# Eight cached sequences in one decoder step: one column tile of TensorE per token, joined window loads, unrolled code

## The chip, the core and the metric

The kernel runs on one NeuronCore of a Trainium2 chip. The metric is the device time of one launch in microseconds (us). The core has TensorE (matrix products; PE in the rows, with its weight loads on a line of their own, PEld), VectorE (DVE), ScalarE (ACT), GpSimd (POOL) and SyncE (SP), whose instruction stream issues most of the DMA transfers. Each engine runs its own instructions in order, and engines wait for each other on semaphores.

## What is computed

One layer of a decoder step for a prompt of 256 tokens and for 8 cached sequences of 4 new tokens each (32 sample tokens). A combined projection gives the inputs of four branches; their outputs are projected, gated and summed, and a gated convolutional MLP follows. The change is in the two attention branches of the 8 cached sequences:

```python
# branch A, group g of three, (window, dilation) = (128,1), (512,4), (2048,16), 2 heads each
kk = concatenate([buf[:, :, 0], k], 1); vv = concatenate([buf[:, :, 1], v], 1)   # cache: W rows x (k,v) x 2 x 128
idx = W + t - j * dilation                                # token t sees taps j = 0..window/dilation
logits = q . kk[idx] + bias[j]; p = softmax over the taps; o = p . vv[idx]
o_A = sum over the groups, weighted by the softmax of their log-sum-exps
# branch B, 4 heads, 1024 cached keys in 8 pages of 128 rows, found through page_table
s = q . mean(keys of a block of 256); the 3 best of 4 blocks stay; softmax over them and the own keys
o_B = p . v
```

All data are f32. Per sequence 8 key pages and 8 value pages of 256 KB each are read, and 1.75 MB of window caches.

## The kernel before

**Order of the whole.** The input projection (about 30 to 316 us), the two small branches C and D, the prompt's attention (to 406 us), then the 8 cached sequences (to 624 us), then gates, output projection and MLP, in which TensorE works without a pause.

**A sequence, on TensorE** (`sample`, L1704). Keys come from the cache with the token on the partition, so every 128x128 piece is turned (`turn`, L1467: a transpose against `ident`) and copied from PSUM by ScalarE (bank 0) or VectorE (bank 1) before it can be multiplied. One sequence issues, in this order: the window keys turned (L1714 to L1733); own-key products of B (L1735) and A (L1742); the first two key groups of the *next* sequence turned (`keys`, L1745); the sliding branch's scores (L1752, L1757, L1761); three more key groups; B's scores of the next sequence, first half (L1695); a key group; the weights `L_b` of B turned, 9 pieces (L1774); two key groups; the weights `L_a` of A turned, 6 pieces (L1782); B's product with the values (L1798); A's (L1804 to L1812); B's result turned (L1819); B's scores of the next sequence, second half; A's result turned (L1826).

**One row set for A.** The sliding branch keeps its 2 heads x 4 tokens as 8 rows. With dilation 4 or 16 token t sees other rows of the cache than token t', so `qs_a` and `pt_a` hold 8 columns for each (head, residue) with zeros where the token does not belong, and 8 products add up into `ps[0:8, 6]`:

```python
for h in range(2):
    for r in range(4):
        c = 48 + 8 * (4 * h + r)
        e.matmul(ps[0:8, 6, 128:256], qs_a[:, c:c + 8], kt_a[:, h, r * P:r * P + P], start=h + r == 0, stop=h + r == 4)
```

B keeps its 4 heads in 4 groups of 32 PSUM partitions, `ps[32 * h:32 * h + 32, ...]`, with 32 weight columns each.

**VectorE and ScalarE.** VectorE's order in a sequence (L1216 to L1288): the copy of window keys, block sums (L1230), scale and bias of B's logits (L1232), the short window's keys (L1221), a key group of the next sequence, the choice of blocks (L1244 to L1250) and the maximum (L1252), A's logits and maximum (L1256 to L1261), and only then the copy of the next sequence's fourth key group (L1264), on which TensorE's L1695 waits. ScalarE copies the even key groups, does the exponentials and scales the results.

**Loads** (`sample_loads`, L502). SyncE reads each page number from SBUF (`value_load`, L481) and issues one DMA of 256 KB (L483), 16 in a sequence. Windows are read in 6 DMAs, 3 for keys and 3 for values (L489 to L493), in rows of 1 KB, into single buffers. The order in a round of the loop is: window keys, 8 key pages of the next sequence, 8 value pages, window values.

**Loop.** Sequences 0 to 6 run as a hardware loop on each engine with counts in registers, the last one as a copy behind it. Ahead of it TensorE makes the bias rows (L1658, L1653) with f32r operands, VectorE copies them to SBUF, and only then (L1670) the first keys are turned.

Of the kernel before, what the change touches and what calls it, by code (L numbers as in the profile page):

```python
# [23 lines left out]
P = 128  # L24
# [111 lines left out]
def build(nc, known, d, o, ctx):  # L136
# [65 lines left out]
    QA = 176  # L202
    qpad_a = sb("qpad_a", [P, NB, QA], F32, R_RAW)
    kv = [sb(f"kv{s}", [P, 4, 512], F32, R_Z + 8192 * s) for s in range(6)]
    bias_b = sb("bias_b", [P, PAST + NB * NS], F32, R_SPLIT)
    bias_a = sb("bias_a", [8, 320 + NB * 96], F32, R_SPLIT + 5120)
# [3 lines left out]
    L_a = sb("L_a", [8, 416], F32, R_SPLIT + 26496)  # L210
    pt_b = sb("pt_b", [P, 9, B_HEADS, 32], F32, R_SPLIT + 9472)
    pt_a = sb("pt_a", [P, 8 + 32 + 32 + 24], F32, R_SPLIT + 28192)
    ob = sb("ob", [P, P], F32, R_SPLIT + 28576)
    oa = sb("oa", [8, 256], F32, R_SPLIT + 29088)
# [50 lines left out]
    win0 = keep("win0", [P, 512])  # L265
    qs_b = keep("qs_b", [P, B_HEADS, 32])
    qs_a = keep("qs_a", [P, QA])
# [26 lines left out]
    kv_landed = [sem(f"kv_landed{s}") for s in range(6)]  # L294
    win_landed = [[sem(f"win{w}_{x}_landed") for w in (1, 2, 0)] for x in ("keys", "values")]
# [56 lines left out]

    def sample_steps(i, last):

        def name(x):
            return ("last", x) if last else x

        def at(count, x, back=0):
            if not last:
                return count.at(x, i, back=back)  # L360
            return count.at(x, NB - 2) if back else count.at(("last", x))
        return name, at


    @block.sync
    def _(sp):
# [106 lines left out]

        sp.wait_ge(pe.sem, pe.at(("PV", NU - 1)))
        sp.wait_ge(dve.sem, dve.at(("P", NU - 1)))
        sp.wait_ge(pool.sem, pool.at("z_own"))
        sp.wait_ge(landed["pages"], 16)

        def page_loads(n, cache, half, slot):
            for q in range(4):  # L480
                page = sp.value_load(pages[0:1, bass.ds(n * NPG + (4 * half + q), 1)], min_val=0,  # L481
                                     max_val=cache.shape[0] - 1)
                sp.dma_start(kv[slot][:, q:q + 1, :], cache[bass.ds(page, 1)].rearrange("a p h e -> p a (h e)"))\  # L483
                    .then_inc(kv_landed[slot], 16)

        def window_loads(i, v):

            cols = slice(256 * v, 256 * v + 256)
            sp.dma_start(kv[2][:, :, cols], d["cache_win1"][0, bass.ds(i, 1), :, v]  # L489
                         .rearrange("a (p r) h e -> p (a r) (h e)", r=4)).then_inc(win_landed[v][0], 16)  # L490
            sp.dma_start(kv[3][0:64, :, cols], d["cache_win2"][0, bass.ds(i, 1), :, v]
                         .rearrange("a (p r) h e -> p (a r) (h e)", r=16)[:, 0:4, :]).then_inc(win_landed[v][1], 16)
            sp.dma_start(win0[:, cols], d["cache_win0"][0, bass.ds(i, 1), :, v].rearrange("a p h e -> p (a h e)"))\  # L493
                .then_inc(win_landed[v][2], 16)

        def next_keys(i, half):

            need = i * 8 + (4 * half + 4)
            if not isinstance(i, int):
                need = sp.snap(sp.to_reg(need))  # L500
                sp.wait_ge(landed["pages"], 16)
            sp.wait_ge(keys_turned, need)  # L502
            page_loads(i + 1, d["cache_k"][0], half, half)

        def sample_loads(i, first, last):
            def used(x):

                return pe.at(x, NB - 2) if last else pe.at(x, i, back=1)
            if not first:
                sp.wait_ge(pe.sem, used(("kTa", 3)))  # L510
            window_loads(i, 0)
            if not last:
                next_keys(i, 0)
                next_keys(i, 1)
            if not first:
                need = used("pv_b")
                if not last:
                    need = sp.snap(sp.to_reg(need))
                    sp.wait_ge(landed["pages"], 16)
                sp.wait_ge(pe.sem, need)  # L520
            for half in range(2):
                page_loads(i, d["cache_v"][0], half, 4 + half)
            if not first:
                sp.wait_ge(pe.sem, used("pv_a"))
            window_loads(i, 1)
        for half in range(2):
            page_loads(0, d["cache_k"][0], half, half)
        sample_loads(0, True, False)
        with sp.Fori(1, NB - 1) as i:
            sample_loads(i, False, False)  # L530
        sample_loads(NB - 1, False, True)


        sp.wait_ge(q_put, 2 * NB)
        with sp.Fori(0, 4) as i:
            for b in range(4):
                for j in range(4):
# [49 lines left out]
    def _(e):  # L587
# [68 lines left out]
        with e.Fori(1, NB) as i:  # L656
            sample_queries(i)
# [1290 lines left out]
```

## Time and profile before

| | us |
|---|---|
| median of 3 runs | 2175.45 (2171.96 to 2177.34) |
| the profiled execution | 2177.7 |
| its span, first to last instruction | 2175.9 |
| TensorE busy, products | 2037.1 (94%) |
| TensorE busy, weight loads | 1927.0 (89%) |
| VectorE busy | 1073.0 (49%) |
| ScalarE busy | 740.7 (34%) |
| GpSimd busy | 81.9 (4%) |

The profiled execution is one run with the hardware profiler; it lasted 1.8 us longer than its span. Its mean granted TensorE clock was 0.969 of full speed. Products are pipelined, so that the busy times of neighbours overlap, and a row's start is a better mark than its end. In the timeline rows an f32 product appears as two records (passes), a transpose as one; "x16" for L1752 is 8 products.

DMA issues in the page: 64 of `cache_k` and 64 of `cache_v` with 256 KB each, and of `cache_win` 16 with 512 KB, 16 with 256 KB and 16 with 128 KB. For one of the 8 sequences that is 16 x 256 + 2 x (512 + 256 + 128) KB = 5888 KB, 6.03 MB.

### The profile page before, as it was taken

The numbers are of one execution on the slowest core, as the hardware profiler recorded it, in microseconds if no ns is written. First come the engines' busy times: TensorE is split into PE (matmuls) and PEld (weight loads), VectorE is DVE, ScalarE is ACT, GpSimd is POOL, SyncE is SP. The second block draws the span as 40 slices with busy tenths as digits, with TensorE's granted clock in tenths as the row PEclk, the third lists the DMA queues.
The fourth block names the chain that finished last, engine by engine and source line by source line (L and its number), as shares of the span: only waits on it lengthen the run. The fifth ranks groups of instructions, "written<-read, shape, count | busy, mean of one in ns | idle before, by whom it ended". The sixth has DMA issues, their size and how long they took to land.

```text
span 2175.9 us, 37737 instructions
## 1 busy us (share of the span) xinstructions
PE 2037.1 (94%) x15329; PEld 1927.0 (89%) x15329; DVE 1073.0 (49%) x1078; ACT 740.7 (34%) x618; POOL 81.9 (4%) x170
## 2 busy tenths in 40 slices
PE   7999996788989999999998969999999999999995
PEld 5999984555569999999998959999999999999994
DVE  4333325434444434444443375656655665665564
ACT  4333332322233333433332424333333333333332
POOL 0000002000000000000000011000000000000001
PEclk9999997899999999999999989999999999999998
DMA  6545522389865454544546514555665565666532
GB/s 233 170 157 171 188 63 72 114 247 244 231 198 170 150 174 157 164 161 159 166 164 193 173 39 156 173 165 193 213 211 206 205 215 202 217 207 216 198 135 59
DMA packets 190741, 377.03 MB, mean 173 GB/s; under 512 B 9849, under 2 KB 34705, under 8 KB 189114
## 3 DMA queue, kind: packets, MB, share of 16 engines
q1 hardware_dynamic: 184412, 340.50, 49.0%
q10 hardware_dynamic: 6247, 35.31, 4.1%
q8 instruction: 66, 1.08, 0.2%
q14 instruction: 16, 0.13, 0.0%
HBM read 365.43 MB, written 37.66 MB: 185 GB/s over the span
## 4 chain that ended last, share of the span: by engine, by line
PE 89%; DVE 5%; ACT 2%; issue 2%; SPq 1%; DMA 1%; ACTq 0%; DVEq 0%
PE ps L1486 26%; PE ps L1488 26%; PE ps L1487 26%; PE ps L1468 4%; PE ps L1474 1%; DVE m_T L1031 1%; PE ps L1798 1%; PE ps L1806 1%; PE ps L1809 1%; PE ps L1695 1%; PE ps L1752 1%; PE ps L1812 1%; PE ps L1637 0%; DVE w_lo L1014 0%; DVE stat L1024 0%
## 5 line engine op out<-in xcount | busy, mean ns | idle before, releaser
L1014 DVE TENSOR_TENSOR w_lo<-w_raw,w_hi 128x2048 fp32r<-128x2048 f32 (+1 forms) x272 | 614.7, 2261 | 786.2 <-ACT w_hi L700 786.2
L1486 PE MATMUL ps<-xn_hi,w_hi 128*128 128x288 f32 x3104 | 917.5, 296 | 27.6 <-DVE xn_lo L1037 13.8
L1488 PE MATMUL ps<-xn_hi,w_lo 128*128 128x288 f32 x3104 | 918.8, 296 | 0.0
L1487 PE MATMUL ps<-xn_lo,w_hi 128*128 128x288 f32 x3104 | 916.9, 295 | 0.0
L700 ACT ACTIVATE w_hi<-w_raw 128x2048 fp32r<-128x2048 f32 (+1 forms) x272 | 514.4, 1892 | 1042.4 <-PE ps L1488 1029.4
L1486 PEld LDWEIGHTS ps<-xn_hi,w_hi 128*128 128x128 f32 x3104 | 585.3, 189 | 32.0 <-DVE xn_lo L1037 15.4
L1487 PEld LDWEIGHTS ps<-xn_lo,w_hi 128*128 128x128 f32 x3104 | 585.1, 189 | 0.0
L1488 PEld LDWEIGHTS ps<-xn_hi,w_lo 128*128 128x128 f32 x3104 | 585.1, 189 | 0.0
L1486 PE MATMUL ps<-act_hi,w_hi 128*128 128x288 f32 x704 | 207.9, 295 | 2.8 <-DVE act_lo L1387 2.8
L1488 PE MATMUL ps<-act_hi,w_lo 128*128 128x288 f32 x704 | 208.5, 296 | 0.0
L1487 PE MATMUL ps<-act_lo,w_hi 128*128 128x288 f32 x704 | 207.9, 295 | 0.0
L1486 PEld LDWEIGHTS ps<-act_hi,w_hi 128*128 128x128 f32 x704 | 132.8, 189 | 3.0 <-DVE act_lo L1387 3.0
L1487 PEld LDWEIGHTS ps<-act_lo,w_hi 128*128 128x128 f32 x704 | 132.8, 189 | 0.0
L1488 PEld LDWEIGHTS ps<-act_hi,w_lo 128*128 128x128 f32 x704 | 132.7, 188 | 0.0
L1394 DVE TENSOR_TENSOR m_T<-ps,m_T 128x1152 f32<-128x1152 f32 x44 | 59.6, 1354 | 54.7 <-PE ps L1488 54.7
L1371 DVE SCALAR_TENSOR_TENSOR hc<-H,conv,hc 128x304 f32<-128x304 f32 x176 | 82.2, 529 | 0.0
L1486 PE MATMUL ps<-M_hi,w_hi 128*128 128x288 f32 x256 | 76.7, 300 | 5.5 <-DVE w_lo L1014 5.5
L1488 PE MATMUL ps<-M_hi,w_lo 128*128 128x288 f32 x256 | 76.7, 300 | 0.0
L1487 PE MATMUL ps<-M_lo,w_hi 128*128 128x288 f32 x256 | 76.6, 299 | 0.0
L1468 PE MATMUL ps<-ident,kv 128*128 128x128 f32 (+1 forms) x384 | 54.8, 282 | 13.4 <-DVE kt_a L1221 6.8
L1468 PEld LDWEIGHTS ps<-ident,kv 128*128 128x128 f32 (+1 forms) x384 | 41.0, 146 | 29.0 <-issue 12.8
L1488 PE MATMUL ps<-O_hi,w_lo 128*128 128x288 f32 x224 | 66.1, 295 | 0.0
(269 smaller groups left out, 1534.7 us busy)
## 6 DMA issues: line engine op xcount, KB each, us to landing
w_raw<-in_w_in SPq DMA_DIRECT2D x104, 1024.0 KB, 5.0
w_raw<-in_w_up SPq DMA_DIRECT2D x88, 1024.0 KB, 5.1
w_raw<-in_w_down SPq DMA_DIRECT2D x44, 1024.0 KB, 5.1
kv<-in_cache_k SPq DMA_DIRECT2D x64, 256.0 KB, 3.5
kv<-in_cache_v SPq DMA_DIRECT2D x64, 256.0 KB, 3.0
w_raw<-in_w_o SPq DMA_DIRECT2D x16, 1024.0 KB, 5.1
out<-in_cache_win ACTq DMA_DIRECT2D x32, 512.0 KB, 4.3
kv<-in_cache_win SPq DMA_DIRECT2D x16, 512.0 KB, 6.4
```

The lines of the kernel that those rows point to most:

```text
L700: e.activation(w_hi[s][:, 0:k, 0:n], w_raw[slot][:, 0:k, 0:n], ACT.Copy).then_inc(hi_ready, 1)
L1014: e.tensor_tensor(w_lo[s][:, 0:k, 0:n], w_raw[slot][:, 0:k, 0:n], w_hi[s][:, 0:k, 0:n].bitcast(F32), ALU.subtract).then_inc(lo_ready, 1)
L1031: e.scalar_tensor_tensor(out=dst[:, c, :], in0=src[:, c, :], scalar=gains[:, g + c:g + c + 1], in1=stat[:, 2, :], op0=ALU.mult, op1=ALU.mult)\
L1371: e.scalar_tensor_tensor(out=dst, in0=src, scalar=w[tap], in1=dst, op0=ALU.mult, op1=ALU.add)\
L1394: e.tensor_tensor(m_T[:, 4 * j:4 * j + 4, :], ps[:, 4 * (j % 2):4 * (j % 2) + 4, 0:TOK], m_T[:, 4 * j:4 * j + 4, :], ALU.add).then_inc(y_a ...
L1468: return e.transpose(dst, src, ident[0:n, 0:n])
L1474: mm = e.matmul(ps[:, bank, 0:TOK], ones[:, :], sq[:, q, k, :], start=q == 0 and k == 0, stop=q == 3 and k == 3)
L1486: e.matmul(dst, w_hi[s][:, r, cols], x_hi[:, k0 + r, :], start=first and r == 0, stop=False)
L1487: e.matmul(dst, w_hi[s][:, r, cols], x_lo[:, k0 + r, :], start=False, stop=False)
L1488: mm = e.matmul(dst, w_lo[s][:, r, cols], x_hi[:, k0 + r, :], start=False, stop=last and r == k - 1)
L1695: mm = e.matmul(ps[32 * h:32 * h + 32, 4 + half, :], qs_b[:, h, :], kt_b[:, half, h, :], start=True, stop=True)
L1752: e.matmul(ps[0:8, 6, 128:256], qs_a[:, c:c + 8], kt_a[:, h, r * P:r * P + P], start=h + r == 0, stop=h + r == 4)
```

## The change

1. **Column tiles.** A's rows move to 4 groups of 32 partitions, one per token, with head h in row 32t + h. Scores, weights times values and the biases each go out as 4 products with 32 weight columns, one per group: own keys 24 products for 6, scores 24 for 18 (8 + 8 + 8 for 8 + 8 + 2), values 16 for 12. `L_a`, `oa`, `bias_a` have 128 partitions for 8. The own values of the three groups are gathered on 96 partitions (`v_own_a`).
2. **Turns of weights.** The turns of `L_b`, `L_a`, `ob`, `oa` become ordinary f32 products against 16, 8 or 4 chosen columns of `ident`; their PSUM rows hold only what is copied on. The pieces of `L_a` are 4 for 6. B's 9 pieces go to one bank, and ScalarE alone copies them.
3. **Loads.** A window is one DMA for keys and values (3 for 6 in a sequence, rows of 2 KB, four in a row for the dilated ones), with two sets of buffers. Keys have 3 half buffers for 2. The first 8 key pages are issued during the prompt's attention. Weights of the next stage load from the end of A's values in sequence 6.
4. **Unrolled.** All 8 sequences are written out on every engine; there is no loop and no register in the waits. GpSimd builds `qs_a` from `z_own` in each sequence.
5. **Start.** A's biases are f32 products in column tiles; TensorE turns the first keys with no wait for VectorE's copies. B's own-key product moves up, between the window's turns.

```diff
-    kv = [sb(f"kv{s}", [P, 4, 512], F32, R_Z + 8192 * s) for s in range(6)]
+    def window_buffers(name, win1_at, win2_at, win0_at):
...
+    k_half = [sb("k_half0", [P, 4, 512], F32, R_Z + 32768), sb("k_half1", [P, 4, 512], F32, R_Z + 40960),
+              sb("k_half2", [P, 4, 512], F32, R_RAW + 16384)]
+    v_half = [sb(f"v_half{s}", [P, 4, 512], F32, R_Z + 8192 * s) for s in range(2)]
...
+        def key_loads(j):
+
+            if j >= 2 * NB:
+                return
+            if j >= 3:
+                sp.wait_ge(keys_turned, 4 * (j - 3) + 4)
+            page_loads(j // 2, d["cache_k"][0], j % 2, k_half[j % 3], k_landed[j % 3])
+
+        def value_loads(n):
+            if n:
+                sp.wait_ge(pe.sem, pe.at(("pv_b", n - 1)))
...
+        def window_loads(n):
...
+            if n >= 2:
+                sp.wait_ge(pe.sem, pe.at(("pv_a", n - 2)))
+            w0, w1, w2 = windows[n % 2]
+            sp.dma_start(w1[:, :, :], d["cache_win1"][0, n].rearrange("(p r) v h e -> p r (v h e)", r=4))\
+                .then_inc(win_landed[n % 2][1], 16)
...
+        sp.wait_ge(dve.sem, dve.at(("oc", 2)))
+        sp.wait_ge(pool.sem, pool.at("z_own"))
+        sp.wait_ge(landed["pages"], 16)
+        key_loads(0)
+        key_loads(1)
         sp.wait_ge(pe.sem, pe.at(("PV", NU - 1)))
         sp.wait_ge(dve.sem, dve.at(("P", NU - 1)))
...
+        sp.wait_ge(pe.sem, pe.at("bias"))
+        window_loads(0)
+        key_loads(2)
+        key_loads(3)
+        value_loads(0)
+        key_loads(4)
+        window_loads(1)
+        for n in range(1, NB):
+            key_loads(2 * n + 3)
+            key_loads(2 * n + 4)
+            value_loads(n)
+            window_loads(n + 1)
...
-            for h in range(2):
-                for r in range(4):
-                    c = 48 + 8 * (4 * h + r)
-                    e.matmul(ps[0:8, 6, 128:256], qs_a[:, c:c + 8], kt_a[:, h, r * P:r * P + P],
-                             start=h + r == 0, stop=h + r == 4)
...
+            for h in range(HPG):
+                for t in range(NT):
+                    e.matmul(ps[32 * t:32 * t + 32, 6, 128:256], qs_a[:, 1, h, t, :], kt_a[:, h, t * P:t * P + P],
+                             start=h == 0, stop=h == 1, skip_group_check=True)
...
-                turn(ps[:, 7 if pg < 4 else 3, pg % 4 * P:pg % 4 * P + P], L_b[:, pg * P:pg * P + P], P)
...
+                e.matmul(ps[:, 3, 16 * pg:16 * pg + 16], L_b[:, pg * P:pg * P + P], row_b,
+                         start=True, stop=True)
...
-            e.matmul(ps[0:8, 6, 0:256], pt_a[:, 0:8], win0[:, 256:512], start=True, stop=False)
-            for r in range(4):
-                e.matmul(ps[0:8, 6, 0:256], pt_a[:, 8 + 8 * r:16 + 8 * r], kv[2][:, r, 256:512],
-                         start=False, stop=False)
...
+            for t in range(NT):
+                e.matmul(ps[32 * t:32 * t + 32, 6, 0:256], pt_a[:, 0, t, :], w0[:, 256:512],
+                         start=True, stop=False, skip_group_check=True)
+            for t in range(NT):
+                e.matmul(ps[32 * t:32 * t + 32, 6, 0:256], pt_a[:, 1, t, :], w1[:, t, 256:512],
+                         start=False, stop=False, skip_group_check=True)
```

How the order moves, at three places of TensorE's stream. Rows with MATMUL name what is written, the moving and the weight operand (`kv_87`, `kv_88` and `k_half_...` are key buffers), and weight columns x moving columns; ISA and REGISTER_ALU rows are the loop's register work.

Scores of the sliding branch, to B's first scores of the next sequence. Before:

```order
L1752 MATMUL ps<-kt_a,qs_a 8x128 x8
L1757 MATMUL ps<-kt_a,qs_a 8x64 x8
L1761 MATMUL ps<-kt_a,qs_a 8x128 x2
L1679 ISA
L1468 MATMUL ps<-ident,kv_87 128x128 x8
L1679 REGISTER_ALU
L1468 MATMUL ps<-ident,kv_88 128x128 x4
L1691 ISA
L1693 REGISTER_ALU
L1695 MATMUL ps<-kt_b,qs_b 32x512 x4
L1468 MATMUL ps<-ident,kv_88 128x128 x4
L1711 ISA
```

With the change:

```order
L1707 MATMUL ps<-kt_a,qs_a 32x128 x8
L1713 MATMUL ps<-kt_a,qs_a 32x64 x8
L1718 MATMUL ps<-kt_a,qs_a 32x128 x8
L1433 MATMUL ps<-ident,k_half_88 128x128 x8
L1433 MATMUL ps<-ident,k_half_86 128x128 x4
L1660 MATMUL ps<-kt_b,qs_b 32x512 x4
L1433 MATMUL ps<-ident,k_half_86 128x128 x4
```

The scores go from 18 products with 8 weight columns to 24 with 32; what follows is unchanged in order.

The turns of the weights, before:

```order
L1468 MATMUL ps<-ident,L_b 128x128 x4
L1773 REGISTER_ALU
L1468 MATMUL ps<-ident,L_b 128x128 x4
L1468 MATMUL ps<-ident,L_b 32x128
L1679 REGISTER_ALU
L1468 MATMUL ps<-ident,kv_88 128x128 x8
L1711 ISA
L1468 MATMUL ps<-ident,L_a 128x8 x2
L1468 MATMUL ps<-ident,L_a 64x8
L1468 MATMUL ps<-ident,L_a 32x8 x3
```

With the change:

```order
L1727 MATMUL ps<-ident,L_b 128x16 x8
L1729 MATMUL ps<-ident,L_b 32x16
L1433 MATMUL ps<-ident,k_half_86 128x128 x8
L1735 MATMUL ps<-ident,L_a 128x8 x2
L1735 MATMUL ps<-ident,L_a 64x8
L1735 MATMUL ps<-ident,L_a 96x8
```

Each turned piece now has 16 or 8 moving columns for 128 or fewer; next keys stay between the two groups.

The sliding branch's values and the results, before:

```order
L1804 MATMUL ps<-win_151,pt_a 8x256
L1806 MATMUL ps<-kv_89,pt_a 8x256 x4
L1809 MATMUL ps<-kv_90,pt_a 8x256 x4
L1812 MATMUL ps<-v_own,pt_a 8x256 x3
L1711 ISA
L1468 MATMUL ps<-ident,ob 128x128
L1688 REGISTER_ALU
L1695 MATMUL ps<-kt_b,qs_b 32x512 x4
L1711 ISA
L1468 MATMUL ps<-ident,oa 128x8 x2
```

With the change:

```order
L1752 MATMUL ps<-win_even,pt_a 32x256 x4
L1755 MATMUL ps<-win_even,pt_a 32x256 x4
L1758 MATMUL ps<-win_even,pt_a 32x256 x4
L1761 MATMUL ps<-v_own_a,pt_a 32x256 x4
L1766 MATMUL ps<-ident,ob 128x16
L1660 MATMUL ps<-kt_b,qs_b 32x512 x4
L1772 MATMUL ps<-ident,oa 128x4 x2
```

12 products of 256 columns become 16, and B's scores of the next sequence stay between the two results.

## Rows read from the trace of the kernel before

**Rows 1.** The core's engines in six stretches: length, busy time (instructions) of each, TensorE clock, DMA share, GB/s.

```profile
424.75:455.87 31.12, 24.50 (x241) 14.25 (x237) 11.06 (x26) 6.29 (x13) 0.54 (x2) 0.89 0.87 251
455.87:480.17 24.30, 21.70 (x239) 13.73 (x237) 11.37 (x28) 6.29 (x13) 0.53 (x2) 1.00 0.88 246
552.93:578.09 25.16, 23.30 (x238) 14.56 (x238) 11.55 (x28) 6.30 (x13) 0.53 (x2) 0.93 0.89 245
557.65:561.00 3.35, 3.35 (x15) 2.19 (x16) 2.06 (x6) 0.00 (x0) 0.00 (x0) 0.50 0.77 229
602.39:623.60 21.21, 17.03 (x191) 11.24 (x190) 8.88 (x24) 4.14 (x9) 0.00 (x0) 0.92 0.86 291
700.00:900.00 200.00, 196.28 (x1477) 195.60 (x1477) 87.63 (x45) 71.77 (x43) 0.00 (x0) 1.00 0.50 163
```

**Rows 2.** TensorE in order of time, third sequence: start, length, line, operation, tiles, idle before and releaser.

```profile
482.66 0.51 PE L1742 MATMUL ps<-z_own,qs_a 128*8 128x32 f32 x12
...
484.74 0.66 PE L1468 MATMUL ps<-ident,kv 128*128 128x128 f32 x4 [0.97 <-DVE kt_a L1221]
485.32 1.92 PE L1752 MATMUL ps<-kt_a,qs_a 128*8 128x128 f32 x16
487.07 1.06 PE L1757 MATMUL ps<-kt_a,qs_a 128*8 128x64 f32 x16
487.97 0.60 PE L1761 MATMUL ps<-kt_a,qs_a 128*8 128x128 f32 x4
...
491.54 1.06 PE L1695 MATMUL ps<-kt_b,qs_b 128*32 128x512 f32 x8 [1.04 <-DVE col L1266]
...
493.03 1.15 PE L1468 MATMUL ps<-ident,L_b 128*128 128x128 f32 x9
...
494.98 0.40 PE L1468 MATMUL ps<-ident,L_a 8*128 8x8 f32 x6
495.30 1.95 PE L1798 MATMUL ps<-kv,pt_b 128*32 128x128 f32 x64
...
497.54 0.60 PE L1804 MATMUL ps<-win,pt_a 128*8 128x256 f32 x2
...
503.00 0.33 PE L1468 MATMUL ps<-ident,ob 128*128 128x128 f32 x1
```

**Rows 3.** VectorE in order of time, same sequence.

```profile
485.43 0.69 DVE L1213 COPY kt_b<-ps 128x512 f32<-128x512 f32 x1 [0.75 <-PE ps L1468]
...
490.54 0.67 DVE L1213 COPY kt_b<-ps 128x512 f32<-128x512 f32 x1
```

**Rows 4.** TensorE in order of time, bias products ahead of the sequences.

```profile
415.75 0.48 PE L1468 MATMUL ps<-ident,kv 128*128 128x128 f32 x1 [1.90 <-DVE bias_b L1206]
```

**Rows 5.** TensorE in order of time, first sequence.

```profile
446.21 1.02 PE L1804 MATMUL ps<-win,pt_a 128*8 128x256 f32 x2 [4.02 <-DMA win<-in_cache_win]
447.02 3.62 PE L1806 MATMUL ps<-kv,pt_a 128*8 128x256 f32 x8
```

**Rows 6.** TensorE in order of time, spatial-gating branch at a clock of 0.50.

```profile
360.00 1.75 PE L1601 MATMUL ps<-wd,vc_tok 32*128 32x32 f32 x8
```

**Rows 7.** TensorE in order of time, last sequence.

```profile
611.82 1.74 PE L1468 MATMUL ps<-ident,L_b 128*128 128x128 f32 x9 [3.20 <-ACT L_b L845]
```

**Rows 8.** SyncE's DMA issues in order of time, inside the loop.

```profile
502.55 8.46 SPq L483 DMA_DIRECT2D kv<-in_cache_v  x8
```

**Rows 9.** SyncE's DMA issues in order of time, the unrolled last sequence.

```profile
596.49 7.96 SPq L483 DMA_DIRECT2D kv<-in_cache_v  x8
604.49 0.58 SPq L489 DMA_DIRECT2D kv<-in_cache_win  x1
...
605.79 0.60 SPq L493 DMA_DIRECT2D win<-in_cache_win  x1
```

**Rows 10.** DMA queues between 430 and 456 us.

```profile
q8 instruction: 2, 0.03, 0.6%
```

More of the change, by code:

```diff
@@ L351, in ffn_unit @@
         return unit_no(U_FFN - 4, 12, i, j)
[L353 to L362, printed above, removed]
     @block.sync
@@ L496, in next_keys @@
[L496 to L525, printed above, removed]
@@ L1763, in sample @@
-            mm.then_inc(pe.sem, pe.step(name("s_a")))
-            if not last:
-                keys(nxt, 2, 5, at)
-                scores(nxt, 0, at)
-                keys(nxt, 5, 6, at)
-            need = value(at(act, "E_b"))
-            e.wait_ge(pool.sem, pool.at("ident"))
-            e.wait_ge(act.sem, need)
-            for pg in range(8):
-                if pg == 4:
-                    e.wait_ge(dve.sem, at(dve, "o_a", back=1))
-                turn(ps[:, 7 if pg < 4 else 3, pg % 4 * P:pg % 4 * P + P], L_b[:, pg * P:pg * P + P], P)
@@ L1775, in sample @@
-            turn(ps[0:NS, 2, P:2 * P], L_b[:, PAST:PAST + NS], P).then_inc(pe.sem, pe.step(name("ptb")))
-            if not last:
-                keys(nxt, 6, 8, at)
-            need = value(at(act, "E_a"))
-            e.wait_ge(pool.sem, pool.at("ident"))
-            e.wait_ge(act.sem, need)
-            turn(ps[:, 6, 416:424], L_a[:, 0:128], 8)
-            turn(ps[:, 6, 424:432], L_a[:, 128:256], 8)
-            turn(ps[0:64, 6, 432:440], L_a[:, 256:320], 8)
-            for g in range(3):
-                mm = turn(ps[0:NS, 6, 440 + 8 * g:448 + 8 * g], L_a[:, 320 + 32 * g:352 + 32 * g], 8)
@@ L1818, in sample @@
-            e.wait_ge(act.sem, need)
-            turn(ps[:, 2, 256:384], ob[:, :], P).then_inc(pe.sem, pe.step(name("otb")))
-            if not last:
-                scores(nxt, 1, at)
-            need = value(at(act, "oa"))
-            e.wait_ge(pool.sem, pool.at("ident"))
-            e.wait_ge(act.sem, need)
-            for h in range(2):
-                mm = turn(ps[:, 2, 432 + 8 * h:440 + 8 * h], oa[:, h * P:h * P + P], 8)
-            mm.then_inc(pe.sem, pe.step(name("ota")))
-        keys(0, 0, 8, None)
@@ L1838, in _ @@
+            mm.then_inc(pe.sem, pe.step(("ota", n)))
+        keys(0, 0, 8)
+        scores(0, 0)
+        scores(0, 1)
+        for n in range(NB):
+            sample(n)
         with e.Fori(0, 4) as i:
```

538 lines of the change are left out of this document (257 added, 281 removed).

## The prediction

> **What bounds the kernel now.** The change touches only the stretch of the eight sequences, 424.75 to 623.6 us, and the bias products ahead of it. I first cut that stretch by sequence [rows 1]: the first takes 31.12 us, a steady one 24.30, the sixth 25.16, the last 21.21. TensorE is busy for 21.7 of 24.3 us, VectorE for 11.4, the DMA engines for 0.88 of the time. So TensorE's order of work sets the pace, with two idle gaps of note in each sequence [rows 2]: 0.97 us before the second key group, on VectorE's copy of window keys, and 1.04 before B's first scores at 491.54, on VectorE again. The second gap ends a chain: VectorE starts on the second key group at 485.43 and works without a wait to the fourth, at 490.54 [rows 3]. From 491.54 on TensorE waits for almost nothing until VectorE's chain can start again with the next window keys. A sequence is therefore one part at VectorE's pace and one at TensorE's, and only what shortens the second part shortens the sequence.
>
> The queue behind them is nearly as full. A round of SyncE has 16 page issues and 6 window issues; it takes 8.46 us from the first to the last of 8 value pages in the loop and 7.96 in the unrolled copy [rows 8, 9].
>
> **Part by part, in a steady sequence.**
>
> *Values of the sliding branch.* Before: 497.54 to 503.00, 5.46 us for 12 products of 256 columns, one behind the other [rows 2]. After: four rounds of four column tiles. The same form stands in the trace: B's 32 products with 128 columns take 1.95 us in rounds of four heads, 0.244 a round; twice the columns give 0.49, and four rounds 1.95. **-3.5 us**, in TensorE's part.
>
> *Scores.* Before 3.2 us (485.32 to 488.5: 487.97 and about 0.53 of its row). After: two rounds of 128 columns, two of 64, two of 128: 1.2. The 2.0 us won lie inside VectorE's chain: the fourth key group still waits for it, and the gap before B's scores grows from 1.04 to about 3.0. **0.** The own-key products of A grow from 6 to 24, in six rounds; they have the 0.97 gap behind them, so even twice their 0.45 us (row 482.66 [rows 2]) costs **0**; were that gap gone, 0.5.
>
> *Turns of the weights.* A turn costs 0.115: from 493.03 to 494.98 there are 17 [rows 2]. An f32 product has two passes, each with a weight load of 128 columns. The nearest row is 8 such passes with 32 moving columns in 1.75 us at half clock [rows 6]: 0.22 a pass, 0.11 at full clock. So `L_b` takes 8 x 0.22 + 0.1 = 1.9 against 1.0, `L_a` (128, 128, 64 and 96 weight columns) about 0.7 against 0.32, `oa` 0.44 against 0.23. **+1.5 us**, all in TensorE's part. The bounds are 0 (a product for a turn at the same price) and twice that.
>
> *Copies.* ScalarE takes over VectorE's share of `pt_b`, two copies of some 0.25 us; two key groups and the turns of `L_a`, 1.7 us, cover them. VectorE has one copy of results for two and four of `pt_a` as before. GpSimd's query copies follow the scores of the sequence before, a whole sequence ahead. **0.**
>
> A steady sequence at full clock: 24.3 - 3.5 + 1.5 = **22.3 us**.
>
> *The clock.* What TensorE did before it fell: after an idle gap of 4.02 us, 8 passes of A's values took 3.62 us [rows 5], where a full clock needs 1.8 (5.46 x 8 / 24); after 3.20 the 9 turns took 1.74 instead of 1.15 [rows 7, 2]; and in the sixth sequence the clock stood at 0.50 for 3.35 us [rows 1], after key turns, little products and the 0.97 gap. There it cost 25.16 - 24.30 = 0.86, because half of the 1.7 us lost ran inside the second gap. With the change, some 5 us of turns and idling (gap 3.0) come right before TensorE's own part, where nothing hides a spell. I take one spell in every other sequence, 1.7 / 2 = **+0.85**: 23.15 us. The Trainium skill (TensorE: Matmul & The Clock Gate, PE-mode transpose) says that transposes do not count as busy for the clock in the same way; by that the new stretch counts as idle throughout, every sequence has its spell, and the rival below holds. The sixth sequence agrees with it, the five without a spell do not settle it.
>
> *SyncE and DMA.* The round is 16 x 1.09 + 1.9 for three window issues = 19.4 us [rows 9], under 22.3; three key halves and two window sets let it run ahead. The waits put into the queue (keys turned, B's values, A's values of two sequences before) hold back only what stands behind them there, and each is over when SyncE gets to it, save the first rounds. DMA: 6.03 MB a sequence at the main stage's 163 GB/s for a share of 0.50, 326 GB/s, is 18.5 us; at the loop's 246 for 0.88 it is 21.6. Either is below 22.3, the second barely.
>
> *The ends.* Keys start with no wait for VectorE's bias copies: 1.90 us idle go [rows 4], two turns and slower f32 biases add 0.8: **-1.1**. The first sequence loses its wait for window values (4.02) and the half clock after it: 31.12 to 23.15, **-8.0**. Sequences 2 to 7: 602.39 - 455.87 = 146.5 to 138.9, **-7.6**. The last: -3.5 + 1.5, and the gap before its turns grows from 3.2 to 5.2, with 0.3 more at half clock: **-1.7**. The next stage's weights are asked for some 20 us before the end of the sequences and need about 10: 0.
>
> **Sum:** -1.1 - 8.0 - 7.6 - 1.7 = -18.4 us on 2177.7. The median of the runs is 2175.45, 2.3 lower; against it I forecast **2157 us**.
>
> **The rivals.**
> - *Full clock throughout* (0.20). The loop's other sequences had it in spite of 2.6 us idle. Then 22.3 us each: -1.1 - 8.8 - 12.7 - 2.0 = -24.6, 2151 us.
> - *A spell in every sequence* (0.18). 24.0 us each: -1.1 - 7.1 - 2.5 - 1.3 = -12.0, 2163 us. The gap of 3.0 is near the 3.20 of [rows 7].
> - *The loads become the bound* (0.08). At the loop's 251 GB/s [rows 1] 6.03 MB take 24.0 us and TensorE waits for values: again about 2163. For it speaks the share of 0.88; against it, that this rate was what TensorE and SyncE asked for, and that rows of 2 KB replace rows of 1 KB.
> - *Slower, by the clock* (0.06). The stretch falls to half and does not recover at once, since turns and gaps go on. At full clock the change is worth 24.6 us, 3.1 a sequence, so it turns when a sequence spends over 6.2 us of TensorE's part at half. With 10 us it loses 5.0 each: -24.6 + 40 = +15, 2191 us.
> - *Unrolled code starves TensorE* (0.02). In 26 us of the first sequence two instruction packets show, at 0.6% of 16 engines 1.25 us each [rows 10]. A sequence has about 600 TensorE instructions; two or three exposed fetches of 1.25 and a queue as long would make it 26 to 28 us: +30, 2205. The Trainium skill (Runtime: NRT & Kernel Launch, Instruction fetch mechanics) says that the sequencer fetches ahead in blocks of 256 instructions and that the cost is mostly hidden; by it this rival gives nothing. The unrolled last sequence shows no such stall.
> - *The tiles do not run side by side*: 16 products of 0.455 are 7.3 us for 5.46, scores 5 for 3.2: some 29 us a sequence, 2215. B's rows in the same form speak against it; it is within the last 0.02.
> - *No measurable change* (0.04): several small losses eat the 18 us.
>
> **The numbers.** Forecast 0.42. Faster by over 0.3% (6.5 us, about what a measurement can tell here): 0.42 + 0.20 + 0.18 + 0.08 = 0.88; within it 0.04; slower 0.08. Low end: full clock, and half of the 1.5 us for the turns not paid (8 x 0.75 = 6), 2145. High end: a spell each and the turns dearer by 0.75, 2170. That leaves out the slower cases and most of "no change".
>
> **What would show it.** Steady sequences of 22.3 us, or 24.0 with a spell of 0.50 in them; A's values 2.0 us; the turns of `L_b` 1.9; an idle gap of some 3 us before B's first scores, ended by VectorE; the first sequence no longer than the others; SyncE's rounds with room between them. A wait for a DMA in steady sequences, turns of `L_b` over 2.5 us, or a gap of another length before B's scores would prove me wrong.

## The result, and the profile after

The changed kernel takes **2187.95 us** (median of 6 runs, 2184.24 to 2189.77) against 2176.94 (median of 6, 2171.96 to 2178.78) on the same chip: ratio 1.0051, 95% interval 1.0036 to 1.0066. It is slower by 11 us where 18 were to be won. The profiled execution lasted 2189.3 us, its span 2187.6 (before 2175.9), its mean granted TensorE clock 0.955 (before 0.969). One run of experiment 7 below, of 2882.75 us at a mean clock of 0.646, is left out of its median.

Each experiment was measured beside the kernel before, on its own chip (medians there 2177.5 to 2178.8), and its ratio is to that kernel. The changed kernel was not repeated there, and the intervals are about 4 us wide to each side, so differences of a few us between two experiments are not told apart.

The stretch of the sequences cut into sequences, from the first own-key product of B of one to that of the next (length, busy time with instructions of PE, PEld, DVE, ACT, POOL, TensorE clock, DMA share, GB/s):

```profile
421.46:448.73 27.27, 23.23 (x307) 17.74 (x306) 11.06 (x25) 6.62 (x15) 0.57 (x3) 0.81 0.94 288
...
530.59:557.87 27.28, 23.17 (x308) 17.74 (x307) 11.05 (x25) 6.57 (x15) 0.57 (x3) 0.81 0.75 224
...
585.13:612.41 27.28, 23.17 (x307) 17.72 (x306) 11.06 (x25) 6.56 (x15) 0.57 (x3) 0.81 0.49 144
```

All seven take 27.3 us with a clock of 0.81, where before five took 24.16 to 24.30 at 1.00 (one of them in [rows 1]). The last of these rows moves only 144 GB/s, since the pages run out there, and is as long as the first with 288: loads are not the bound. The same view of the second sequence, one microsecond a row:

```profile
458.00:459.00 1.00, 0.13 (x4) 0.16 (x8) 0.84 (x3) 1.00 (x5) 0.00 (x0) 1.00 0.66 274
459.00:460.00 1.00, 1.00 (x9) 0.16 (x5) 0.00 (x0) 0.43 (x1) 0.00 (x0) 1.00 1.01 344
460.00:461.00 1.00, 1.00 (x7) 1.00 (x7) 0.13 (x1) 0.00 (x0) 0.00 (x0) 0.53 1.15 311
...
469.00:470.00 1.00, 1.00 (x26) 0.94 (x20) 0.00 (x0) 0.00 (x0) 0.00 (x0) 0.50 0.92 277
470.00:471.00 1.00, 1.00 (x32) 0.65 (x24) 0.00 (x0) 0.00 (x0) 0.00 (x0) 0.85 0.82 260
471.00:472.00 1.00, 1.00 (x24) 0.42 (x16) 0.00 (x0) 0.37 (x1) 0.00 (x0) 1.00 0.90 328
```

The clock falls at about 460.1 and is back at 470.3: **10.2 us at half clock** (0.50 in the rows), with TensorE busy all the time. I call such a stretch a spell. Each of the seven sequences has one. What TensorE does in it, in order of time (start, length, line, operation, tiles, idle before and releaser):

```profile
452.28 0.66 PE L1433 MATMUL ps<-ident,k_half 128*128 128x128 f32 x4 [1.00 <-DVE kt_a L1202]
452.86 0.65 PE L1707 MATMUL ps<-kt_a,qs_a 128*32 128x128 f32 x16
453.32 0.41 PE L1713 MATMUL ps<-kt_a,qs_a 128*32 128x64 f32 x16
453.55 0.62 PE L1718 MATMUL ps<-kt_a,qs_a 128*32 128x128 f32 x16
...
458.87 1.06 PE L1660 MATMUL ps<-kt_b,qs_b 128*32 128x512 f32 x8 [2.71 <-issue]
459.87 0.97 PE L1433 MATMUL ps<-ident,k_half 128*128 128x128 f32 x4
460.63 3.43 PE L1727 MATMUL ps<-ident,L_b 128*128 128x16 f32 x16
463.99 0.29 PE L1729 MATMUL ps<-ident,L_b 128*32 128x16 f32 x2
464.21 1.97 PE L1433 MATMUL ps<-ident,k_half 128*128 128x128 f32 x8
465.98 1.59 PE L1735 MATMUL ps<-ident,L_a 128*128 128x8 f32 x8
467.50 3.30 PE L1747 MATMUL ps<-v_half,pt_b 128*32 128x128 f32 x64
...
471.08 0.64 PE L1752 MATMUL ps<-win_odd,pt_a 128*32 128x256 f32 x8
...
473.22 0.39 PE L1766 MATMUL ps<-ident,ob 128*128 128x16 f32 x2
```

The sliding branch's scores take 1.24 us (452.86 to 454.10), so the gap ahead of B's first scores, 1.04 before [rows 2], is 2.71. The releaser is given as "issue", but VectorE's copy of the fourth key group ended just ahead (VectorE in order of time; [rows 3] before):

```profile
458.09 0.68 DVE L1194 COPY kt_b<-ps 128x512 f32<-128x512 f32 x1
```

B's scores still run at full clock, and the fall comes within the key group behind them (0.97 us for 0.66). The turns of `L_b` as products, two key groups, the turns of `L_a` and most of B's values run at half. A's values, after the spell, take 2.14 us (471.08 to 473.22) against 5.46.

Time at half clock is counted below in one way for every kernel: the granted clock of 420 to 620 us in steps of 0.5 us, each step's share under 1.00 taken twice. A spell that an edge of the stretch cuts counts with what lies inside. Before it is **14.8 us**, after **71.7**. A microsecond at half does half a microsecond's work, so that 56.9 us more are worth some 28 us. Expected and measured change of the profiled execution differ by 18.4 + 11.6 = 30.

### The profile page after: what moved, and what is told of

Its sections match the earlier page's. It is cut to its first block, busy times and chain, and to the rows that moved or that the text cites. A ratio compares the mean times of both kernels' runs of the same rounds, so it can differ in the third digit from the quotient of the medians.

```text
span 2187.6 us, 38132 instructions
## 1 busy us (share of the span) xinstructions
PE 2041.9 (93%) x15921; PEld 1953.5 (89%) x15921; DVE 1068.8 (49%) x1049; ACT 743.5 (34%) x628; POOL 80.5 (4%) x170
## 4 chain that ended last, share of the span: by engine, by line
PE 90%; DVE 5%; issue 2%; ACT 2%; ACTq 0%; DMA 0%; SPq 0%; DVEq 0%
PE ps L1451 26%; PE ps L1453 26%; PE ps L1452 26%; PE ps L1433 4%; PE ps L1747 1%; PE ps L1727 1%; PE ps L1439 1%; DVE m_T L1018 1%; PE ps L1660 1%; PE ps L1735 1%; DVE col L1212 0%; PE ps L1602 0%; DVE L_b L1214 0%; DVE w_lo L1001 0%; DVE stat L1011 0%
## 5 line engine op out<-in xcount | busy, mean ns | idle before, releaser
L1452 PE MATMUL ps<-O_lo,w_hi 128*128 128x288 f32 x224 | 66.0, 294 | 0.0
L1451 PE MATMUL ps<-O_hi,w_hi 128*128 128x288 f32 x224 | 65.9, 294 | 0.0
```

Of the source, the lines that this page charges most:

```text
L1451: e.matmul(dst, w_hi[s][:, r, cols], x_hi[:, k0 + r, :], start=first and r == 0, stop=False)
L1452: e.matmul(dst, w_hi[s][:, r, cols], x_lo[:, k0 + r, :], start=False, stop=False)
```

## The experiments

Theory A: column-tiled scores end early, TensorE idles 2.7 us in VectorE's chain, and the clock falls there. Theory A2: the products that replaced the turns keep it from coming back. Rivals: the products alone do it; or something else (loads, unrolled code) takes the time and the clock is a side show. All experiments but the sixth start from the changed kernel.

**1. The gap filled with products.** `ones` times `ident` into unused columns, whose results nobody reads.

```diff
             if n + 1 < NB:
+                for k in range(11):
+                    e.matmul(ps[:, 7, 256:384], ones[:, :], ident[:, :], start=True, stop=True)
                 scores(n + 1, 0)
```

> The changed kernel with 11 extra f32 products of ones by the identity (128 columns each, some 2.4 us at full clock, into PSUM columns that nobody reads) in TensorE's gap ahead of B's first scores, in sequences 1 to 7. The outputs stay the reference's. Theory A (the idle gap of 2.7 us, with turns around it, drops the clock, and the 10 us at half clock behind it cost the time): the clock stays at 1.00 in steady sequences, the turns of L_b take 1.9 us for 3.4, a sequence takes 22.2 to 22.5 us for 27.3, and the kernel some 33 to 38 us less than the changed one: about 2152. Theory B (the new products that turn the weights, 128 weight columns against 16 moving ones, are slow or drop the clock by themselves, whatever the gap): turns of L_b still 3.4 us, 27.3 us a sequence, about 2188.

2162.63 us (2160.60 to 2164.82), ratio to the kernel before 0.9927 (0.9910 to 0.9943). Sequences, by the same view; five of seven stand at 1.00:

```profile
469.01:491.59 22.58, 20.93 (x329) 15.78 (x328) 11.05 (x25) 6.55 (x15) 0.58 (x3) 1.00 1.01 329
...
537.59:561.79 24.20, 22.56 (x330) 17.14 (x329) 11.05 (x25) 6.56 (x15) 0.57 (x3) 0.93 0.80 227
```

More work on TensorE makes the kernel 25 us faster, less than the 33 to 38 expected. Time at half clock: 27.3 us. So the clock was most of the loss, and without the idle gap most sequences have no spell. A sequence of the change at full clock is 22.58 us.

The gap is not the only thing that goes before a spell. The sixth and seventh sequences, filled like the others, have one of 3.4 us each. In the sixth it begins at 553.0, with B's values, 5.3 us behind the last idle piece, which was 0.26 us long (TensorE in order of time):

```profile
547.73 1.07 PE L1660 MATMUL ps<-kt_b,qs_b 128*32 128x512 f32 x8 [0.26 <-issue]
...
553.02 3.43 PE L1749 MATMUL ps<-v_half,pt_b 128*32 128x128 f32 x64
```

**2. `L_b` turned by transposes again.** The nine turns as before, VectorE copying its share; the gap stays. `L_a`'s pieces move to another bank.

```diff
-                e.matmul(ps[:, 3, 16 * pg:16 * pg + 16], L_b[:, pg * P:pg * P + P], row_b,
-                         start=True, stop=True)
+                turn(ps[:, 7 if pg < 4 else 3, pg % 4 * P:pg % 4 * P + P], L_b[:, pg * P:pg * P + P], P)
```

> The changed kernel with one part undone: L_b is turned by 9 transposes of 128 columns into two banks again, and VectorE copies its share of pt_b. The gap stays. [...] Rival (the length of the spell has nothing to do with the form of the turns; transposes do no more for the clock): the spell stays about 10 us and only the turns' own 0.9 us at full clock, up to 1.8 at half, are won: 25.5 to 26.5 us a sequence, about 2178.

2157.47 us (2155.06 to 2159.91), ratio 0.9902 (0.9885 to 0.9918); 34.1 us at half clock. In its third sequence, TensorE in order of time:

```profile
483.16 1.20 PE L1663 MATMUL ps<-kt_b,qs_b 128*32 128x512 f32 x8 [2.71 <-issue]
484.29 1.12 PE L1436 MATMUL ps<-ident,k_half 128*128 128x128 f32 x4
485.19 2.13 PE L1436 MATMUL ps<-ident,L_b 128*128 128x128 f32 x9
487.12 1.17 PE L1436 MATMUL ps<-ident,k_half 128*128 128x128 f32 x8
...
489.04 1.96 PE L1751 MATMUL ps<-v_half,pt_b 128*32 128x128 f32 x64
```

Behind the same gap the clock falls (nine turns in 2.13 us for 1.15), but it is back by 487, after 3.42 us. Of six spells in 420 to 620, one lasts 10.2. Two sequences have the gap of 2.71 and no spell at all; they take 21.56 us at 1.00.

The run is faster than the 2165 to 2172 us that I had put beside theory A2. Some 8 us of its gain on the change are the turns' own price, 22.58 - 21.56 in each sequence, and not the clock.

**3. The gap shortened from the other side.** VectorE's copy of the fourth key group moves ahead of the two maxima and A's logits.

```diff
+            odd_keys(n + 1, 3)
...
-            odd_keys(n + 1, 3)
```

> The changed kernel with VectorE's copy of the fourth key group put ahead of the maximum of B's logits and of A's logits, behind the choice of blocks. TensorE's gap ahead of B's first scores should shrink from 2.7 to about 0.5 us, with a new one of about 1 us ahead of the turns of L_b. Theory A: with no gap near 3 us the clock stays up; a sequence takes 20.7 to 21.5 us, the kernel about 2142 to 2150. Theory B (the turns' form): still at half clock there, 25.5 to 26 us, about 2176.

2166.68 us (2162.71 to 2170.18), ratio 0.9949 (0.9929 to 0.9969). It lies between the two forecasts. One sequence at full clock takes 21.27 us; six are at 0.80 to 0.94, and 58.0 us are spent at half. The gap of 2.71 is now two, 0.37 and 0.76 (TensorE in order of time, third sequence):

```profile
478.43 1.06 PE L1660 MATMUL ps<-kt_b,qs_b 128*32 128x512 f32 x8 [0.37 <-issue]
479.42 0.66 PE L1433 MATMUL ps<-ident,k_half 128*128 128x128 f32 x4
480.84 2.29 PE L1727 MATMUL ps<-ident,L_b 128*128 128x16 f32 x16 [0.76 <-ACT L_b L834]
...
485.04 1.59 PE L1735 MATMUL ps<-ident,L_a 128*128 128x8 f32 x8
```

So a long gap is not needed: with the products in place the clock falls even here. Theory A alone is too simple.

**4. Both: the copy ahead and `L_b` turned by transposes.** The edits of 2 and 3 together.

> The two edits before together: the copy ahead, and L_b turned by transposes. Theory A: the clock stays up and the turns cost 1.0 us for 1.9: 20 to 20.7 us a sequence, unless SyncE's round of 19.4 us or the loads bind; about 2136 to 2145. If transposes count less for the clock than products, the clock falls here and not in the run with the copy ahead alone, and this one is the slower of the two.

2146.68 us (2144.77 to 2148.41), ratio 0.9852 (0.9836 to 0.9869). Five sequences take 20.35 us at 1.00. The run is 2 us over the expected range, and the first sequence is long, for a load (the view of sequences, then TensorE in order of time):

```profile
423.82:450.38 26.56, 18.94 (x299) 13.03 (x298) 11.34 (x27) 6.78 (x14) 0.57 (x3) 0.91 0.92 295
...
491.57:511.92 20.35, 17.83 (x298) 12.24 (x298) 11.34 (x27) 6.45 (x14) 0.57 (x3) 1.00 0.94 304
```

```profile
448.48 1.97 PE L1436 MATMUL ps<-ident,win_odd 128*128 128x128 f32 x8 [5.16 <-DMA win_odd<-in_cache_win]
```

With 3, this separates the two edits: the same two short gaps, and no spell in five sequences once the products are gone.

**5. More moving columns in `L_b`'s products.** 64 columns of `ident` for 16; the 48 further results are not read.

```diff
-                e.matmul(ps[:, 3, 16 * pg:16 * pg + 16], L_b[:, pg * P:pg * P + P], row_b,
+                e.matmul(ps[:, 3, 64 * pg:64 * pg + 64], L_b[:, pg * P:pg * P + P], row_w,
```

> The change with L_b turned into 16 products of 64 moving columns instead of 16 (the extra 48 columns are further rows of the identity and are not read; own keys go to a bank of their own). The idle piece of 2.7 us ahead of the second sequence's first scores stays. If few moving columns are what holds the clock at half for 10.2 us in every sequence, the spell ends sooner, at some 3.4 to 6.8 us: 23.5 to 25.5 us a sequence instead of 27.27, a run of 2162 to 2176 us. If the form of these products does not matter, or if only their duration does (some 2 us more on TensorE), the spell stays 10 us: 27 us a sequence or more, 2186 to 2195 us.

2186.59 us (2175.05 to 2193.80), ratio 1.0034 (1.0014 to 1.0055): as slow as the change, with spells of 10.24 us. Its third sequence, and from its fourth, at half clock, the turns of `L_b`:

```profile
473.66:500.98 27.32, 23.21 (x307) 17.64 (x307) 11.06 (x25) 6.57 (x15) 0.58 (x3) 0.81 0.77 242
```

```profile
512.66 3.52 PE L1728 MATMUL ps<-ident,L_b 128*128 128x64 f32 x16
```

Between 16 and 64, the number of moving columns is not the cause; my first reading of A2 falls. These 16 passes take 3.52 us against 3.43 for 16 columns, so the moving columns do not set their price. The weight load, which the prediction named, has 128 columns in both; no run changed it.

**6. The products alone.** The kernel before, with its loop and its gap of 1.04, but `L_b` turned by products.

```diff
-                turn(ps[:, 7 if pg < 4 else 3, pg % 4 * P:pg % 4 * P + P], L_b[:, pg * P:pg * P + P], P)
+                e.matmul(ps[:, 7 if pg < 4 else 3, 64 + 16 * (pg % 4):80 + 16 * (pg % 4)],
+                         L_b[:, pg * P:pg * P + P], row_b, start=True, stop=True)
```

> The kernel before, in which only L_b's keys are turned by 16 products of 16 columns; scores stay as they were, so TensorE's idle piece ahead of the second sequence's first scores stays near 1.0 us, and the loop of two bodies stays. If the idle piece of 2.7 us is needed to let the clock fall, no long spells come: about 25.1 us a sequence (24.30 and some 0.8 for slower turns), 2180 to 2188 us with clock 1.00 in nearly every sequence. If the narrow products let the clock fall by themselves, the sequences show 0.80 to 0.90 and 27 us or more: over 2195 us.

2184.58 us (2182.70 to 2189.51), ratio 1.0033 (1.0020 to 1.0047). Two of its sequences:

```profile
532.45:557.76 25.31, 22.71 (x246) 14.71 (x245) 11.35 (x29) 6.28 (x14) 0.53 (x2) 1.00 0.83 236
...
583.09:609.96 26.87, 24.23 (x246) 15.29 (x245) 11.35 (x29) 6.28 (x14) 0.53 (x2) 0.94 0.68 185
```

A sequence at full clock is 25.3 us for 24.30: the turns' own price, 1.0, near the forecast 0.9. Time at half clock is 12.3 us, no more than the 14.8 of the kernel before, and no spell is longer than 3.4. But there are more of them: three of the seven sequences have one, where before one of the six behind the first had, and I had expected 1.00 in nearly every sequence. So the products by themselves bring no long spells and at most a few short ones; with the changed scores around them they go with 10.2 us in each.

**7. The gap filled with transposes.** As 1, with 21 transposes of `ident`.

```diff
+                for k in range(21):
+                    turn(ps[:, 7, 256:384], ident[:, :], P)
```

> The change with the idle piece of 2.7 us filled by 21 transposes of the identity (some 2.4 us) instead of by the 11 products of 128 columns of the first experiment. If transposes keep the clock up as products do, the result is that of the first experiment, 2160 to 2166 us, most sequences at clock 1.00 and 22.6 us. If transposes do not count for the clock, the spell of 10.2 us stays in every sequence: 27.3 us each, 2185 to 2192 us.

2163.85 us (2158.43 to 2168.45), ratio 0.9925 (0.9902 to 0.9948), as with products in experiment 1. Its fifth sequence:

```profile
521.84:544.43 22.59, 20.77 (x329) 15.58 (x328) 11.06 (x25) 6.58 (x15) 0.57 (x3) 1.00 0.92 248
```

Five of seven sequences stand at 1.00 and 27.3 us are spent at half, as in experiment 1. Transposes hold the clock up here as products do. The Trainium skill (TensorE: Matmul & The Clock Gate, PE-mode transpose), which the prediction weighed, says that transposes do not count as busy in the same way; in this run 2.46 us of nothing else in each gap had the same effect as 2.62 us of products. For this gap the page and the measurement differ, and the measurement decides.

**8. The fourth with earlier loads.** The second sequence's windows and half of the first's values are issued ahead of the wait for the biases.

```diff
+        window_loads(1)
+        value_loads(0, (0,))
         sp.wait_ge(pe.sem, pe.at("bias"))
...
-        value_loads(0)
+        value_loads(0, (1,))
...
-        window_loads(1)
```

> The fourth experiment (copy of the odd keys ahead of the maxima, and L_b turned by transposes) with the first sequence's value half and the second sequence's windows issued before the wait for the bias. The fourth lost 5.16 us in waiting for the second sequence's windows. If that wait is only the late issue, it goes: the first-to-second step falls from 26.56 to 20.5 to 21.5 us and the run from 2146.7 to 2139 to 2143 us. If the transfers of that stretch are bound by the bandwidth, the wait moves to another load and the time stays at 2145 to 2148 us.

2141.47 us (2138.70 to 2145.60), ratio 0.9827 (0.9801 to 0.9853): the lowest median of all, though its interval overlaps that of experiment 4. The wait of 5.16 is gone, and with it the 10.2 us at half behind it. A wait of 2.45 us for key pages at 427.26, with a spell of 3.4, stands in the first sequence instead. That sequence takes 22.87 us where experiment 4 had 26.56 and 20.5 to 21.5 were expected; the steady ones are the same.

```profile
422.79:445.66 22.87, 19.20 (x298) 13.58 (x297) 11.34 (x27) 6.52 (x14) 1.07 (x3) 0.93 0.86 284
...
486.37:506.73 20.36, 17.83 (x299) 12.23 (x298) 11.35 (x27) 6.47 (x14) 0.57 (x3) 1.00 0.89 270
```

**9. Transposes for as long as the products.** Experiment 2 with eight of its nine transposes issued twice, the second onto the first.

```diff
             for pg in range(8):
...
-                turn(ps[:, 7 if pg < 4 else 3, pg % 4 * P:pg % 4 * P + P], L_b[:, pg * P:pg * P + P], P)
+                for k in range(2):
+                    turn(ps[:, 7 if pg < 4 else 3, pg % 4 * P:pg % 4 * P + P], L_b[:, pg * P:pg * P + P], P)
```

> The second experiment (L_b turned by nine transposes, the idle piece of 2.7 us left) with eight of the transposes issued twice, so that they take as long as the 16-column products did. The second experiment had spells of 3.4 and 6.8 us where the change has 10.2. If the form of the turns (a product against a transpose) decides how long a spell lasts, the spells stay short: 23.5 to 24.5 us a sequence and 2164 to 2172 us. If the length of a sequence and the place of the idle piece in it decide, the spells of 10.2 us come back: 27.3 us a sequence and 2184 to 2192 us.

2166.43 us (2165.12 to 2166.92), ratio 0.9943 (0.9927 to 0.9960). Its fourth sequence:

```profile
494.52:518.59 24.07, 19.96 (x307) 14.31 (x306) 11.35 (x27) 6.46 (x14) 0.57 (x3) 0.93 0.91 258
```

Each sequence has one spell of 3.4 us and takes 24.1: the prediction's second rival (24.0) in pure form. TensorE has the work of the changed kernel in length and the same gap, and differs in the form of `L_b`'s turns (and in who copies them): the spell lasts a third.

**10. Neither: transposes and a filled gap.** The edits of 1 and 2 together.

> The second experiment with the gap filled as in the first: neither the idle piece nor the narrow products. If the half-clock time is the whole of what the change lost, nearly every steady sequence stands at clock 1.00 with 21.5 to 21.8 us, time at half clock in 420 to 620 us falls under 20 us and the run is 2144 to 2152 us. If something else takes time too, it stays at the 2157 us of the second experiment.

2154.66 us (2151.79 to 2157.22), ratio 0.9886 (0.9869 to 0.9902): slower than expected. Three sequences take the expected 21.56 or 21.60 at 1.00, but 30.7 us are spent at half, not under 20, and the 3 us by which it is ahead of experiment 2 are within the intervals. Two spells of 3.4 us follow waits for loads, 1.40 us at 427.72 and 1.01 at 492.09, and the last sequence has two of 6.8. One of 10.2 begins at 557.5, behind a break within the products of one line, for which no semaphore accounts (TensorE in order of time):

```profile
554.29 0.62 PE L1764 MATMUL ps<-win_odd,pt_a 64*32 64x256 f32 x2
556.02 0.63 PE L1764 MATMUL ps<-win_odd,pt_a 64*32 64x256 f32 x6 [1.11 <-issue]
556.58 0.64 PE L1767 MATMUL ps<-v_own_a,pt_a 96*32 96x256 f32 x8
```

So spells also follow other idle pieces than the one that was filled.

**11. The gap half filled.** As 1, with 5 products.

> The change with 5 products of 128 columns in the gap instead of 11, so that some 1.5 us of the 2.7 stay idle. The kernel before held its clock in most sequences with 1.04 us idle there. If the length of the idle piece decides, 1.5 us lets spells through in some sequences: 2165 to 2178 us. If any filling is enough, 2160 to 2165 us as in the first experiment; if none but a full one helps, 10.2 us spells in every sequence and 2185 to 2190 us.

2163.39 us (2160.47 to 2172.49), ratio 0.9934 (0.9915 to 0.9952); 27.3 us at half clock. With 0.85 to 1.60 us still idle, by sequence, it is as good as the full filling (TensorE in order of time, third sequence):

```profile
480.46 1.06 PE L1660 MATMUL ps<-kt_b,qs_b 128*32 128x512 f32 x8 [1.32 <-issue]
481.46 0.66 PE L1433 MATMUL ps<-ident,k_half 128*128 128x128 f32 x4
481.95 1.86 PE L1729 MATMUL ps<-ident,L_b 128*128 128x16 f32 x16
```

**All of them together** (a spell is a piece at half clock in 420 to 620 us; the stretch takes in the last sequence, with its gap of some 4 us, and in the faster kernels the pause of 4.6 us ahead of the next stage; a spell cut by an edge is not in the column of spells):

| | ahead of B's scores | `L_b` turned by | sequence at clock 1.00 | at half clock | longest spell, how often | median us |
|---|---|---|---|---|---|---|
| before | idle 1.04 | 9 transposes | 24.16 to 24.30 | 14.8 | 6.8 x1 | 2177 |
| changed | idle 2.71 | products | none | 71.7 | 10.2 x7 | 2188 |
| 1 | filled, 0.26 idle | products | 22.58 | 27.3 | 10.2 x2 | 2163 |
| 7 | filled, 0.42 idle | products | 22.59 | 27.3 | 10.2 x1 | 2164 |
| 11 | idle 0.85 to 1.60 | products | 22.58 | 27.3 | 10.2 x1 | 2163 |
| 6 | idle 1.04 | products (kernel before) | 25.3 | 12.3 | 3.4 x3 | 2185 |
| 5 | idle 2.7 | products, 64 columns | 22.63 | 66.5 | 13.7 x1, 10.2 x5 | 2187 |
| 2 | idle 2.71 | 9 transposes | 21.56 | 34.1 | 10.2 x1 | 2157 |
| 9 | idle 2.71 | 17 transposes | none | 39.8 | 10.2 x1, 3.4 x7 | 2166 |
| 10 | filled, 0.25 idle | 9 transposes | 21.56 | 30.7 | 10.2 x1 | 2155 |
| 3 | idle 0.37 and 0.76 | products | 21.27 | 58.0 | 13.7 x1, 10.2 x1 | 2167 |
| 4 | idle 0.37 and 0.76 | 9 transposes | 20.35 | 27.3 | 10.2 x2 | 2147 |
| 8 | idle 0.37 and 0.76 | 9 transposes | 20.35 | 30.7 | 10.2 x2 | 2141 |

## Why the prediction was wrong

**The step that failed** is the one on the clock: "I take one spell in every other sequence, 1.7 / 2 = +0.85". It was a spell in every sequence, and not of 3.4 us but of 10.2. The steps of the sequence on TensorE, VectorE and the queues came out; at 27.28 us against 23.15 a sequence is off by 4.1 us, 28.9 in seven, nearly the whole of the 30 that the forecast is off. The clock's term is 3.85 of it (4.7 lost for 0.85), 27 us in all; the other 0.28 a sequence is the sum at full clock.

- *Values of A, -3.5:* 2.14 us where 1.95 were forecast, so -3.3. *Scores, 0:* right, and the gap came out at 2.71 for the forecast 3.0. *Turns, +1.5:* `L_b` 1.95 us at full clock (481.95 to 483.9 in experiment 11) for 1.9, `L_a` some 0.9 for 0.7. *Full-clock sequence:* 22.58 for 22.3, seen in experiments 1, 7 and 11.
- *The turns were priced for their length only.* Going from products back to transposes of the same length (experiment 9) gives 21 us; that edit's effect on the clock had no term in the sum. The gap was named as a cause and had a term of one spell in two sequences; filling it gives 25 us. Each of the two edits undone alone gives back most of the loss: it takes both to have 10.2 us in every sequence.
- *The mechanism was among the rivals*, "slower, by the clock", with 10 us at half, 5.0 lost in each sequence and 2191 us, at a chance of 0.06. Measured: 10.2 us, 27.27 - 22.58 = 4.7 lost, 2188. For its low chance stood only the length of the spell in the sixth sequence, 3.4 us. But that trace held a longer one too: 6.8 us at half from 445 on, beginning within the 4.02 us wait [rows 5], which the forecast took away with the wait. And right ahead of the sequences, from 404.1 to 421.1, it stands at half for 17.1 us, in the bias products and the first key turns, with TensorE busy for most of it (the view of stretches, kernel before):

```profile
405.00:410.00 5.00, 4.54 (x15) 3.32 (x15) 0.81 (x2) 0.28 (x1) 3.13 (x13) 0.50 0.32 89
```

- *"The new stretch counts as idle throughout"* does not fit the change either: `L_b`'s turns in it are products, and going back to transposes made the spells shorter, not longer (experiments 2 and 9).
- *SyncE and DMA, 0:* right, though [rows 9] give 1.00 us for a page issue (596.49 to 604.49 for 8) and so a round of 17.9 us, not 1.09 and 19.4. The rate fell from 288 to 144 GB/s between rows of equal length. *The ends:* the first windows are turned at 420.44 for 424.75, -4.3, of which 2.05 are already there when the bias products start and the rest is the wait of 1.90 [rows 4] with what surrounds it; forecast -1.1. *The last sequence* took 27.0 us to the next stage's first product for 25.9 before, +1.2 where -1.7 was forecast: its gap of 3.98 (forecast 5.2) was followed by turns at half clock, in the first row below (TensorE, last sequence; [rows 7] before), and B's values behind them ran at half too.

```profile
620.59 3.60 PE L1727 MATMUL ps<-ident,L_b 128*128 128x16 f32 x16 [3.98 <-ACT L_b L834]
...
626.02 3.64 PE L1747 MATMUL ps<-v_half,pt_b 128*32 128x128 f32 x64
```

- *Starved TensorE:* not in the changed kernel, whose 7 "issue" waits in the stretch all stand ahead of B's scores; but its variants show stops of such a kind, whose cause no run shows (last section). *Tiles one behind the other:* no, 48 passes of own keys went through in 0.63 us.

**What stays open.** Why a spell that begins in one of these stretches ends after 3.4 us in one kernel and after 10.2 in the next, with TensorE busy without a break in both. Experiment 9 says that the form of `L_b`'s turns matters, 5 that its moving columns do not, 6 that the products alone bring no long spells. But experiments 2, 4, 8, 9 and 10, which turn `L_b` by transposes, have one or two spells of 10.2 us as well: they begin within the last sequence's gap of 4 us (4, 8, 9), within waits of 3.06 and 5.16 us for window loads (2, 4), and some 1.5 us behind a break of 0.86 and 1.11 us within A's values (8 and 10). Nor is it shown why a spell begins where it does: two sequences of experiment 2 have the full gap and none, two of experiment 1 have one with hardly any idle time near. The length of a sequence also differs between these kernels, so that the place of the gap within the clock's own course is not excluded as a cause; experiment 9 comes nearest, and its sequences are 24.1 us for 27.3. `L_a`'s turns as transposes were not tried in the changed kernel, nor the loads and the unrolling alone.

## What to carry to other kernels

When an edit shortens TensorE's work ahead of a wait for another engine, the time does not vanish: it becomes an idle gap, and its price can be the clock afterwards, here 4.7 us in 27. So count in the trace of before *every* spell at half clock with its length, the longest included, and carry that as the size of the risk.

In this kernel the remedy was to put the other engine's releasing instruction earlier (VectorE's copy ahead of the maxima) and to keep the turns of `L_b` as transposes. With both, the same column tiles and joined loads give 2147 us for 2177, and 2141 with the first loads issued earlier. The earlier copy alone left 58 us at half. Filling the idle TensorE time with work that nobody reads gave 2163.

## What the runs showed of the hardware

- Useless work makes this kernel faster: 11 products or 21 transposes in a gap of 2.7 us take 24 to 25 us off the run of the changed kernel, 5 products as much.
- The spells at half clock within 420 to 620 us lasted 3.4, 6.8 or 10.2 us, and 13.7 once each in experiments 3 and 5. In the changed kernel the clock stayed at half for 10.2 us while TensorE was busy for 1.00 of every microsecond (460 to 470).
- An f32 pass with 128 weight columns takes 0.21 to 0.22 us at half clock with 16 moving columns as with 64 (3.43 and 3.52 us for 16), and 0.116 at full clock (1.86 us): a transpose takes 0.115 to 0.13 (21 in 2.46 us, 9 in 1.20). A product of two such passes costs about two transposes.
- In seven of the ten unrolled variants TensorE stops once to three times for 0.16 to 1.67 us between products of the sliding branch or B's values, and the profile gives no releaser; neither the loop kernels (before, experiment 6) nor the changed kernel do. The longest, 1.67 us, is in experiment 7 at 563, and makes a sequence at clock 1.00 take 24.65 us for 22.59. The loading of the longer code might explain it; no run isolated that.
- The changed kernel and experiment 5, at 27.27 and 27.32 us a sequence, kept that length to 0.06 us while their DMA rate fell from 288 to 144 and from 242 to 144 GB/s.
